# Differential attention in an encoder layer: weights times values as three reduced-precision products on split operands, most of it one unit later

## The chip, the cores and the metric

The kernel runs on one core of a Trainium2 chip. The metric is the device time of one launch in microseconds (us); lower is better. PE is the matmul engine TensorE (PEld its weight loads), ACT is ScalarE, DVE is VectorE, POOL is GpSimd, SP is the queue that issues transfers.

## What is computed

One encoder layer on two sequences of 272 and 1040 tokens (16 meta tokens and 256 or 1024 others). Each layer projects the input, runs a linear recurrence on half of the width and differential attention on the other half, and ends in a projection and a feed-forward part. The change touches only the attention:

```
q, k: 4 heads x 2 components x 64      v: 4 heads x 128
s    = einsum('bqhcd,bkhcd->bhcqk', q, k)
pr   = softmax(s)                      # each component by itself
amap = pr[:, :, 0] - lam * pr[:, :, 1]
o    = einsum('bhqk,bkhe->bqhe', amap, v)
```

## The kernel before

The layer is a row of stages, each a block in which every engine has its own instruction list, written out in program order; engines meet only through semaphores, and a waiting instruction holds up all that stands behind it on its engine. `attention` is one of these stages. It goes through 40 units, each one head and 128 query rows: per head two units of the short sequence (272 keys, "short units") and then eight of the long one (1040 keys, "long units"). Unit k does this:

- **score** (PE, L1949): two components, 64 rows each, into pS0 and pS1, three PSUM banks each; the last 16 keys go to the third bank. It waits until both exponentials of unit k-1 have been read out of pS (`exped`).
- **largest** (DVE, L2039): the negated maximum of each component. **exp** (ACT, L1995): exponential and row sum, from pS to pr.
- **difference** (DVE, L2046, L2047, L2050): two small instructions on the row sums and one over the whole row, pr0 + s * pr1, in place.
- **turn** (PE, L1962): the row is transposed in tiles of 128 keys, in batches: batch 0 is tiles 0 to 3 into pT, batch 2 is tiles 7 and 8 (8 has 16 keys) into pT, batch 1 is tiles 4 to 6 into the free part of pS0's third bank, once exp 0 of the next unit has read it. A short unit has one batch of three tiles.
- **copy** (ACT L1916 for batch 0; DVE L1916 and L1919 for batches 2 and 1): from PSUM to amT.
- **times_v** (PE, L1972): the turned tiles times v, in plain float32, summed in pO. The profile writes such a product as two records. **out_of** (ACT, L2006): pO to o_rows.

POOL works through an independent triangular solve (`substitute`) beside the first three quarters of the stage. Nothing but the two small loads at its start comes by DMA. PE's order is score(k), turn(k-1, 0), times_v(k-1, 0), turn(k-1, 2), turn(k-1, 1), times_v(k-1, 2), times_v(k-1, 1), and then score(k+1). ACT's is the copy of batch 0 of k-1, exp(k, 0), exp(k, 1), out_of(k-1). DVE's is difference(k-1), largest(k, 0), largest(k, 1), the copies of batches 2 and 1 of k-1.

`three_pass` (L220) is a helper that other stages use: both operands are kept as a rounded high part and a rest, both of type float32r, and a product is low*high + high*low + high*high, three matmuls of one record each (L223, L224, L225).

## Time and profile before

| | us |
|---|---|
| median of 3 runs | 2192.63 |
| lowest, highest | 2190.95, 2195.10 |
| the profiled execution, its own time | 2195.91 |
| span of the profile | 2193.9 |

| engine | busy us | share of the span |
|---|---|---|
| PE | 2001.2 | 91% |
| PEld | 1669.4 | 76% |
| DVE | 1411.3 | 64% |
| ACT | 969.2 | 44% |
| POOL | 349.7 | 16% |

The profile shows one execution. Around its span lie 2.0 us that its own time holds as well. Busy time is a sum over stages with different limits, so a share says little on one stage; the rows below are of the attention stage, which lies from about 650 to 926 us, and of a stretch of the projection before it.

### The profile page before, as it was taken

The page shows a single profiled execution, that of the slowest core. Times are in us where ns is not written, and L with a number is a line of the kernel's source. Part 1 is how long each engine was busy: PE and PEld are TensorE (multiplying, and loading weights), DVE is VectorE, ACT ScalarE, POOL GpSimd, SP SyncE. Part 2 cuts the span into 40 slices and gives each one's busy share as a digit, 9 for nine tenths or more (in the row PEclk, how much of TensorE's full clock was granted, in tenths as well). Part 3 has the DMA queues.
Part 4 walks back from the last instruction along what each step waited for, and adds up shares of the span by engine and source line. Part 5 has one row for each costly group of instructions (what it writes and reads, how often), then busy time and mean ns, then how long its engine had stood idle before and what let it go on. Part 6 is the DMA issues. An engine that isn't in the chain of part 4 may idle for free. (4 is left out here: it accounts for less than half of the span.)

```text
span 2193.9 us, 40726 instructions
## 1 busy us (share of the span) xinstructions
PE 2001.2 (91%) x16199; PEld 1669.4 (76%) x16199; DVE 1411.3 (64%) x2299; ACT 969.2 (44%) x1792; POOL 349.7 (16%) x354
## 2 busy tenths in 40 slices
PE   5999999997778888787999698899999999999999
PEld 4666777775555555576887487899999999988887
DVE  5877666673866776655777646756655565557566
ACT  7454467783744444453454322422232232333433
POOL 0000000000019994164554200000000000000000
PEclk8999999998778999958999899899999999999999
DMA  4111155657940001038884534122222222295343
GB/s 179 66 45 54 56 192 203 219 203 245 276 136 1 1 1 58 28 117 170 195 186 115 174 126 142 35 100 93 105 81 87 82 100 81 83 357 168 98 148 109
DMA packets 147287, 269.63 MB, mean 123 GB/s; under 512 B 12992, under 2 KB 85568, under 8 KB 144800
## 3 DMA queue, kind: packets, MB, share of 16 engines
q1 hardware_dynamic: 147104, 267.09, 38.2%
q8 instruction: 127, 2.08, 0.4%
q14 instruction: 56, 0.46, 0.1%
HBM read 172.53 MB, written 91.54 MB: 120 GB/s over the span
## 5 line engine op out<-in xcount | busy, mean ns | idle before, releaser
L2942 DVE TENSOR_TENSOR ff_lefts<-normed_raw,ff_lefts 128x512 fp32r<-128x512 f32 x154 | 105.6, 687 | 97.9 <-ACT ff_lefts L2826 97.7
L225 PE MATMUL ff_acc<-right_t_high,ff_lefts 128*128 128x320 f32 x528 | 163.1, 309 | 0.0
L224 PE MATMUL ff_acc<-right_t_low,ff_lefts 128*128 128x320 f32 x528 | 163.1, 309 | 0.0
L223 PE MATMUL ff_acc<-right_t_high,ff_lefts 128*128 128x320 f32 x528 | 163.1, 309 | 0.0
L223 PE MATMUL ff_acc<-normed_nl 128*128 128x512 f32 x385 | 149.8, 389 | 0.0
L225 PE MATMUL ff_acc<-normed_nl,normed_nh 128*128 128x512 f32 x385 | 149.8, 389 | 0.0
L2826 ACT CAST ff_lefts<-normed_raw 128x512 fp32r<-128x512 f32 x154 | 93.3, 619 | 116.1 <-DMA normed_raw<-in_w_up 56.1
L2852 ACT COPY normed_n<-ff_acc 128x640 f32<-128x640 f32 x66 | 45.9, 695 | 205.6 <-PE ff_acc L225 204.5
L1972 PE MATMUL at_pO<-heads_vt,at_amT 128*128 128x128 f32 (+1 forms) x624 | 104.6, 302 | 35.0 <-ACT at_amT L1916 24.5
L1972 PEld LDWEIGHTS at_pO<-heads_vt,at_amT 128*128 128x128 f32 (+1 forms) x624 | 82.8, 195 | 61.0 <-issue 39.9
L3014 DVE TENSOR_TENSOR normed_nl<-normed_raw,normed_nh 128x640 fp32r<-128x640 f32 x77 | 63.3, 822 | 91.7 <-ACT normed_nh L2875 91.5
L2875 ACT CAST normed_nh<-normed_raw 128x640 fp32r<-128x640 f32 x77 | 56.3, 731 | 144.7 <-PE ff_acc L225 126.2
L223 PE MATMUL ff_acc<-normed_nh,ff_lefts 128*128 128x320 f32 x352 | 109.9, 312 | 7.5 <-DVE ff_lefts L2942 7.5
L223 PE MATMUL pj_acc<-parts_nh,pj_w0rest 128*128 128x512 f32 (+1 forms) x288 | 110.2, 383 | 7.1 <-DVE parts_nl L800 7.1
L2039 DVE TENSOR_REDUCE at_st<-at_pS 128x1 f32<-128x1040 f32 (+1 forms) x80 | 82.7, 1076 | 49.8 <-PE at_pS L1949 49.4
L224 PE MATMUL ff_acc<-normed_nl,ff_lefts 128*128 128x320 f32 x352 | 109.6, 311 | 0.0
L225 PE MATMUL ff_acc<-normed_nh,ff_lefts 128*128 128x320 f32 x352 | 109.6, 311 | 0.0
L223 PE MATMUL pj_acc<-parts_nh,pj_w1rest 128*128 128x512 f32 (+1 forms) x288 | 108.3, 376 | 0.0
L224 PE MATMUL pj_acc<-parts_nl,pj_w0high 128*128 128x512 f32 (+1 forms) x288 | 105.3, 366 | 0.0
L633 ACT COPY pj_raw<-pj_acc 128x512 f32<-128x512 f32 (+1 forms) x72 | 37.4, 523 | 153.4 <-PE pj_acc L225 152.0
L225 PE MATMUL pj_acc<-parts_nh,pj_w0high 128*128 128x512 f32 (+1 forms) x288 | 105.1, 365 | 0.0
L224 PE MATMUL pj_acc<-parts_nl,pj_w1high 128*128 128x512 f32 (+1 forms) x288 | 104.5, 363 | 0.0
(372 smaller groups left out, 5684.5 us busy)
## 6 DMA issues: line engine op xcount, KB each, us to landing
normed_raw<-dram_h SPq DMA_DIRECT2D x77, 320.0 KB, 3.0
ch_ops<-dram_sx SPq DMA_DIRECT2D x88, 256.0 KB, 5.3
dram_sx<-pr_sx SPq DMA_DIRECT2D x16, 1024.0 KB, 4.1
dram_h<-normed_spread_h SPq DMA_DIRECT2D x44, 320.0 KB, 2.3
pj_packed<-in_w_in SPq DMA_DIRECT2D x24, 512.0 KB, 5.0
heads_vt<-dram_sx SPq DMA_DIRECT2D x44, 256.0 KB, 4.9
normed_raw<-in_w_gate SPq DMA_DIRECT2D x22, 512.0 KB, 4.3
normed_raw<-in_w_up SPq DMA_DIRECT2D x22, 512.0 KB
```

The costliest lines, as they stand in the source:

```text
L223: nc.tensor.matmul(out, ll, rh, start=start, stop=False, skip_group_check=onto_kept)
L224: nc.tensor.matmul(out, lh, rl, start=False, stop=False, skip_group_check=onto_kept)
L225: return nc.tensor.matmul(out, lh, rh, start=False, stop=stop, skip_group_check=onto_kept)
L633: nc.scalar.copy(raw[p % 2][:, CUTS[n]:CUTS[n + 1]], acc[bank_of(i)][:, 0:widths[n]]).then_inc(copied, 1)
L1972: last = mm(pO[:, out_cols(k)], amT[k % 2][0:kn, w, :], g.vt[0:kn, h, v0 + w, :], start=(w == 0), stop=(w == tiles_of[k][min(1, batches[k] ...
L2039: nc.vector.reduce_max(st[k % 2][:, x, 0:1], pS[x][:, 0:ln], AX_X, negate=True).then_inc(maxed[x], 1)
L2826: nc.scalar.copy(lefts[:, q % LEFTS, 0, :], raw[:, y, QUARTER[p], :]).then_inc(high, 1)
L2852: nc.scalar.copy(in_two(to), got(y, p)).then_inc(kept, 1)
L2875: nc.scalar.copy(left_high[s], left_raw[s]).then_inc(left_cut, 1)
L2942: tt(lefts[:, q % LEFTS, 1, :], raw[:, y, QUARTER[p], :], lefts[:, q % LEFTS, 0, :].bitcast(F32), ALU.subtract).then_inc(low, 1)
L3014: tt(left_low[s], left_raw[s], left_high[s].bitcast(F32), ALU.subtract).then_inc(left_rest, 1)
```

## The change

- The two amT buffers become am_high and am_low, two of each, in float32r. ACT now takes all batches out of PSUM with a rounding copy into am_high (`high_part`, order 0, 2, 1); DVE then reads the same PSUM tile again and subtracts am_high from it into am_low (`low_part`).
- v is split in the same way, once a head: `cut_v` on ACT, four rounding copies, `rest_v` on DVE, four subtractions.
- `times_v` calls `three_pass`: three matmuls for each tile.
- Batches 2 and 1 of unit k-2 are multiplied behind score(k) and turn(k-1, 0), one unit later than before. Batch 0 of k-1 follows behind them.
- ACT's out_of(k-2) now stands ahead of exp(k, 0). high_part of batches 2 and 1 stands behind exp(k, 1). DVE's low_part(k-1, 0) stands between the two maxima.
- New waits on PE: the last piece of score(k) waits until batch 1 of k-2 is split, turn(k-1, 0) waits until batch 2 of k-2 is split (they share a bank), times_v(k, 0) waits for out_of(k-1) and for v's rest.

```diff
-        amT = [c.sb(f"amT{s}", (P, 9, P)) for s in range(2)]
+        am_high, am_low = ([c.sb(f"{n}{s}", (P, 9, P), F32R) for s in range(2)] for n in ("am_high", "am_low"))
+        v_high, v_low = (c.sb(n, (P, 2, len(VTILES), P), F32R) for n in ("v_high", "v_low"))
...
         def copied(eng, k, b):
-            if b == 0:
-                eng.wait_ge(act_copied, PRIMED + act0[k] + 1)
-            else:
-                eng.wait_ge(tail_copied, PRIMED + dve0[k] + AFTER[b])
+            eng.wait_ge(low_made, PRIMED + bat0[k] + AFTER[b] + 1)
...
                     for lo in range(0, ln, 512):
                         hi = min(lo + 512, ln)
+                        if lo == 1024 and k >= 2 and batches[k - 2] > 1:
+                            copied(pe, k - 2, 1)
...
                     if b == 0:
                         pe.wait_ge(diffed, PRIMED + k + 1)
+                        if k:
+                            copied(pe, k - 1, 2 if batches[k - 1] > 1 else 0)
...
                     if b == 0:
-                        pe.wait_ge(ocopied, PRIMED + k - 1)
+                        pe.wait_ge(ocopied, PRIMED + k)
+                        pe.wait_ge(v_rest, PRIMED + h + 1)
                     copied(pe, k, b)
                     for w in tiles_of[k][b]:
                         kn = min(P, ln - w * P)
-                        last = mm(pO[:, out_cols(k)], amT[k % 2][0:kn, w, :], g.vt[0:kn, h, v0 + w, :],
-                                  start=(w == 0), stop=(w == tiles_of[k][min(1, batches[k] - 1)][-1]))
+                        last = three_pass(nc, pO[:, out_cols(k)], [t[k % 2][0:kn, w, :] for t in (am_high, am_low)],
+                                          [t[0:kn, h % 2, v0 + w, :] for t in (v_high, v_low)],
+                                          w == 0, w == tiles_of[k][min(1, batches[k] - 1)][-1])
...
-                for k in range(1, ALL + 1):
+                for k in range(1, ALL + 2):
                     if k < ALL:
                         score(k)
-                    if k:
+                    if k <= ALL:
                         turn(k - 1, 0)
+                    if k > 1 and batches[k - 2] > 1:
+                        times_v(k - 2, 2)
+                        times_v(k - 2, 1)
+                    if k <= ALL:
                         times_v(k - 1, 0)
                         if batches[k - 1] > 1:
                             turn(k - 1, 2)
                             turn(k - 1, 1)
-                            times_v(k - 1, 2)
-                            times_v(k - 1, 1)
...
+                def high_part(k, b):
+                    act.wait_ge(turned, PRIMED + bat0[k] + AFTER[b] + 1)
                     if b == 0:
                         act.wait_ge(outs, PRIMED + k - 1)
+                    copy_batch(lambda of, got: nc.scalar.copy(of(am_high), got), k, b).then_inc(high_made, 1)
+
+                def cut_v(h):
+                    for of, at in v_runs(h):
+                        last = nc.scalar.copy(v_high[at], g.vt[of])
+                    last.then_inc(v_cut, 1)
...
-                for k in range(ALL + 1):
-                    if k:
-                        turn_copy(k - 1, 0)
+                for k in range(ALL + 2):
+                    if 1 <= k <= ALL:
+                        high_part(k - 1, 0)
+                    if k >= 2:
+                        out_of(k - 2)
                     if k < ALL:
                         exp(k, 0)
                         exp(k, 1)
...
-                    if k:
-                        out_of(k - 1)
+                    if k % NU == 0 and k < ALL:
+                        cut_v(k // NU)
+                    if 1 <= k <= ALL and batches[k - 1] > 1:
+                        high_part(k - 1, 2)
+                        high_part(k - 1, 1)
...
+                def low_part(k, b):
+                    dve.wait_ge(high_made, PRIMED + bat0[k] + AFTER[b] + 1)
+                    copy_batch(lambda of, got: nc.vector.tensor_tensor(of(am_low), got, of(am_high).bitcast(F32), ALU.subtract), k, b
+                               ).then_inc(low_made, 1)
+
+                def rest_v(h):
+                    dve.wait_ge(v_cut, PRIMED + h + 1)
+                    for of, at in v_runs(h):
+                        last = nc.vector.tensor_tensor(v_low[at], g.vt[of], v_high[at].bitcast(F32), ALU.subtract)
+                    last.then_inc(v_rest, 1)
...
                     if k < ALL:
                         largest(k, 0)
+                    if k:
+                        low_part(k - 1, 0)
+                    if k < ALL:
                         largest(k, 1)
...
-                    if k and by_dve[k - 1]:
-                        tail(k - 1)
+                    if k % NU == 0 and k < ALL:
+                        rest_v(k // NU)
+                    if k and batches[k - 1] > 1:
+                        low_part(k - 1, 2)
+                        low_part(k - 1, 1)
```

How this moves PE's instructions, in the inner long units. Digits behind names number the buffers; at_pr10 is the row of the odd units, at_pr00 of the even ones. Before, from turn(k-1, 0) to the first piece of score(k+1):

```order
L1962 MATMUL at_pT<-at_ident,at_pr10 128x128 x4
L1972 MATMUL at_pO<-heads_vt,at_amT1 128x128 x4
L1962 MATMUL at_pT<-at_ident,at_pr10 128x128
L1962 MATMUL at_pT<-at_ident,at_pr10 16x128
L1962 MATMUL at_pS0<-at_ident,at_pr10 128x128 x3
L1972 MATMUL at_pO<-heads_vt,at_amT1 128x128 x5
L1949 MATMUL at_pS0<-heads_kr,heads_qr 128x512
```

Now, from turn(k-1, 2) of an odd unit to the first products behind the next score:

```order
L1968 MATMUL at_pT<-at_ident,at_pr10 128x128
L1968 MATMUL at_pT<-at_ident,at_pr10 16x128
L1968 MATMUL at_pS0<-at_ident,at_pr10 128x128 x3
L1953 MATMUL at_pS0<-heads_kr,heads_qr 128x512
L1953 MATMUL at_pS1<-heads_kr,heads_qr 128x512
L1953 MATMUL at_pS0<-heads_kr,heads_qr 128x512
L1953 MATMUL at_pS1<-heads_kr,heads_qr 128x512
L1953 MATMUL at_pS0<-heads_kr,heads_qr 128x16
L1953 MATMUL at_pS1<-heads_kr,heads_qr 128x16
L1968 MATMUL at_pT<-at_ident,at_pr00 128x128 x4
L223 MATMUL at_pO<-at_v_high,at_am_low1 128x128
L224 MATMUL at_pO<-at_v_low,at_am_high1 128x128
```

The products of a unit's last five tiles (am_low1, am_high1: the odd unit) moved behind the next score and the next unit's first four transposes.

ACT, same place in the program, before (first_y_first is o_rows here, the output of a unit):

```order
L2006 COPY first_y_first<-at_pO 128x128
L1916 COPY at_amT0<-at_pT 128x512
L1995 ACTIVATE at_pr10,first_z0<-at_pS0,at_st1 128x1040
L1995 ACTIVATE at_pr11,at_st1<-at_pS1,at_st1 128x1040
L2006 COPY first_y_first<-at_pO 128x128
```

and now:

```order
L2021 COPY first_y_first<-at_pO 128x128
L2005 ACTIVATE at_pr10,first_z0<-at_pS0,at_st1 128x1040
L2005 ACTIVATE at_pr11,at_st1<-at_pS1,at_st1 128x1040
L2012 CAST at_am_high0<-at_pT 128x128
L2012 CAST at_am_high0<-at_pT 16x128
L2012 CAST at_am_high0<-at_pS0 128x384
L2012 CAST at_am_high1<-at_pT 128x512
L2021 COPY first_y_first<-at_pO 128x128
```

The copy of a unit's output moved from behind the two exponentials to ahead of them, and three more copies stand behind them.

## Rows read from the trace of the kernel before

**Rows 1.** Busy time by stretch: us, engines, PE's granted clock, DMA share, GB/s

```profile
650.00:926.20 276.20, 228.74 (x1352) 154.61 (x1352) 186.88 (x304) 117.47 (x250) 183.20 (x188) 0.93 0.03 13
```

**Rows 2.** PE in time order, one long unit: start, length, instruction, idle before

```profile
686.55 2.12 PE L1949 MATMUL at_pS<-heads_kr,heads_qr 64*128 64x512 f32 x12
688.59 0.66 PE L1962 MATMUL at_pT<-at_ident,at_pr 128*128 128x128 f32 x4
690.02 1.13 PE L1972 MATMUL at_pO<-heads_vt,at_amT 128*128 128x128 f32 x8 [0.77 <-ACT at_amT L1916]
...
691.93 1.77 PE L1972 MATMUL at_pO<-heads_vt,at_amT 128*128 128x128 f32 x10
693.63 2.12 PE L1949 MATMUL at_pS<-heads_kr,heads_qr 64*128 64x512 f32 x12
```

**Rows 3.** ACT in time order, the same unit

```profile
689.29 0.59 ACT L1916 COPY at_amT<-at_pT 128x512 f32<-128x512 f32 x1 [2.37 <-PE at_pT L1962]
689.97 1.13 ACT L1995 ACTIVATE at_pr<-at_pS,at_st 128x1040 f32<-128x1040 f32 x1
691.12 1.13 ACT L1995 ACTIVATE at_pr<-at_pS,at_st 128x1040 f32<-128x1040 f32 x1
692.14 0.19 ACT L1995 ACTIVATION_READ_ACCUMULATOR at_pr<-at_pS,at_st 128x1 f32 x1
693.74 0.27 ACT L2006 COPY first_y_first<-at_pO 128x128 f32<-128x128 f32 x1 [1.40 <-PE at_pO L1972]
```

**Rows 4.** DVE in time order, the same unit

```profile
688.69 2.39 DVE L2039 TENSOR_REDUCE at_st<-at_pS 128x1 f32<-128x1040 f32 x2 [1.34 <-PE at_pS L1949]
691.40 0.29 DVE L1916 COPY at_amT<-at_pT 128x128 f32<-128x128 f32 x1 [0.32 <-PE at_pT L1962]
691.82 0.56 DVE L1916 COPY at_amT<-at_pS 128x384 f32<-128x384 f32 x1
692.44 0.16 DVE L2046 RECIPROCAL at_st<-at_st 128x1 f32<-128x1 f32 x1
692.94 1.41 DVE L2050 SCALAR_TENSOR_TENSOR at_pr<-at_pr,at_st 128x1040 f32<-128x1040 f32 x1
```

**Rows 5.** Weight loads in time order, in the projection stage

```profile
485.00 0.75 PEld L557 LDWEIGHTS pj_pair<-lora_small,pr_q 128*128 128x128 f32 x6
485.67 0.19 PEld L223 LDWEIGHTS pj_acc<-parts_nh,pj_w1rest 128*128 128x128 f32 x1
485.78 0.19 PEld L224 LDWEIGHTS pj_acc<-parts_nl,pj_w1high 128*128 128x128 f32 x1
```

**Rows 6.** PE in time order, three_pass on 288 columns

```profile
486.44 0.30 PE L225 MATMUL pj_acc<-parts_nh,pj_w1high 128*128 128x288 f32 x1
486.58 0.30 PE L223 MATMUL pj_acc<-parts_nh,pj_w1rest 128*128 128x288 f32 x1
```

**Rows 7.** Groups by line and shape: count, busy us, mean ns, idle before

```profile
L2942 DVE TENSOR_TENSOR ff_lefts<-normed_raw,ff_lefts 128x512 fp32r<-128x512 f32 x154 | 105.6, 687 | 97.9 <-ACT ff_lefts L2826 97.7
L2050 DVE SCALAR_TENSOR_TENSOR at_pr<-at_pr,at_st 128x1040 f32<-128x1040 f32 x32 | 49.1, 1533 | 1.1
L804 DVE TENSOR_TENSOR pj_w0rest<-pj_packed,pj_w0high 128x1024 fp32r<-128x1024 f32 x12 | 14.7, 1222 | 11.2 <-ACT pj_w0high L624 11.2
L624 ACT CAST pj_w0high<-pj_packed 128x1024 fp32r<-128x1024 f32 x12 | 12.6, 1046 | 0.0
```

**Rows 8.** Busy time by stretch, columns as in Rows 1: four stretches

```profile
787.59:793.30 5.71, 4.70 (x33) 3.50 (x32) 3.42 (x9) 1.80 (x6) 5.24 (x7) 1.00 0.02 4
793.30:796.23 2.93, 2.23 (x14) 1.37 (x13) 0.92 (x3) 1.72 (x7) 2.69 (x4) 1.00 0.00 0
866.79:877.57 10.78, 10.01 (x40) 6.91 (x40) 6.28 (x11) 2.82 (x6) 0.00 (x0) 0.57 0.01 2
877.57:884.65 7.08, 6.17 (x40) 4.22 (x39) 4.97 (x9) 3.22 (x6) 0.00 (x0) 1.00 0.00 0
```

More of the change, by code:

```diff
@@ L1885, in attention @@
         diffed, outs, ocopied = c.sem("diffed"), c.sem("outs"), c.sem("ocopied")
-        turned, act_copied, tail_copied = c.sem("turned"), c.sem("act_copied"), c.sem("tail_copied")
+        turned, high_made, low_made = c.sem("turned"), c.sem("high_made"), c.sem("low_made")
         tiles_of = [[range(0, 4), range(4, 7), range(7, 9)] if u[3] == LEN_B else [range(0, 3)] for u in units]
         batches = [len(x) for x in tiles_of]
-        by_act = [min(n, 1) for n in batches]
-        by_dve = [n - a for n, a in zip(batches, by_act)]
-        bat0, act0, dve0 = ([sum(x[:k]) for k in range(ALL)] for x in (batches, by_act, by_dve))
+        bat0 = [sum(batches[:k]) for k in range(ALL + 1)]
         row_sum = lambda k, x: st[k % 2][:, 1, 1:2] if x else g.z0[:, units[k][0], k % NU:k % NU + 1]
@@ L1915, in copy_batch, with v_runs @@
             n = full - tiles.start
-            last = copy(amT[k % 2][:, tiles.start:full, :], src[:, 0:n * P].rearrange("p (w t) -> p w t", w=n))
+            at = lambda t, rows, lo, hi: t[k % 2][rows, lo:hi, :]
+            last = copy(lambda t: at(t, slice(0, P), tiles.start, full), src[:, 0:n * P].rearrange("p (w t) -> p w t", w=n))
             if full < tiles.stop:
                 kn = ln - full * P
-                last = copy(amT[k % 2][0:kn, full, :], turned_tile(b, full)[0:kn, :])
+                last = copy(lambda t: at(t, slice(0, kn), full, full + 1), turned_tile(b, full)[0:kn, :].rearrange("p (w t) -> p w t", w=1))
             return last
+        def v_runs(h):
+            return [((slice(0, n), h, slice(w0, w1)), (slice(0, n), h % 2, slice(w0, w1))) for w0, w1, n in VRUNS]
         with nc.Block() as block:
@@ L1996, in exp @@
                                          bias=st[k % 2][:, x, 0:1], accum_out=row_sum(k, x)).then_inc(exped[x], 1)
-                def turn_copy(k, b):
-                    act.wait_ge(turned, PRIMED + bat0[k] + b + 1)
+                def high_part(k, b):
+                    act.wait_ge(turned, PRIMED + bat0[k] + AFTER[b] + 1)
                     if b == 0:
                         act.wait_ge(outs, PRIMED + k - 1)
-                    copy_batch(nc.scalar.copy, k, b).then_inc(act_copied, 1)
+                    copy_batch(lambda of, got: nc.scalar.copy(of(am_high), got), k, b).then_inc(high_made, 1)
[3 more added lines that the diff above has]
+                    last.then_inc(v_cut, 1)
                 def out_of(k):
@@ L2051, in difference @@
                                                    op0=ALU.mult, op1=ALU.add).then_inc(diffed, 1)
-                def tail(k):
-                    for b in (2, 1):
-                        dve.wait_ge(turned, PRIMED + bat0[k] + AFTER[b] + 1)
-                        copy_batch(nc.vector.tensor_copy, k, b).then_inc(tail_copied, 1)
+                def low_part(k, b):
[7 more added lines that the diff above has]
+                    last.then_inc(v_rest, 1)
                 for k in range(ALL + 1):
```

1 line of the change is left out of this document (added).

## Prediction

> **What bounds the stage now.** I read the stretch table first, to see how long the attention stage is and at what clock it runs; then PE, ACT and DVE in time order over one long unit, to see which engine never catches its breath; then, for prices, the groups by line and shape, and the weight loads and narrow matmuls of another stage.
>
> The stage takes some 276 us at a mean clock of 0.93 [rows 1]. In the inner long units it repeats exactly: score starts at 686.55 and again at 693.63, a period of 7.08 us [rows 2]. PE sets it. Its list for one unit is the score (2.04), four transposes, a wait of 0.77 for ACT's copy, eight records of products, five transposes, ten records of products, and the next score starts at once, though both exponentials had been done at 692.33 [rows 2, 3]. ACT waits 2.37 and 1.40 us a unit for PE, DVE 1.34 and 0.32 [rows 3, 4]. So PE's list is the bound, with about 1.4 us of waits and unhidden starts in it, and ACT and DVE have slack. The question is what closes the loop once the products move.
>
> **PE's own work.** A product is now two records, 0.112 us from start to start: eight of them last 1.13 with a tail of 0.16 and an unhidden start [rows 2]. What holds them at 0.112 seems to be the weight load, not the columns: six records of only 2 columns, each with 128 columns of weights, have loads that start (0.75 - 0.19) / 5 = 0.112 apart, and two float32r loads behind one another start at 485.67 and 485.78, also 0.11 apart [rows 5]. At full clock 128 columns stream in 0.053. No float32r matmul in the trace is narrower than 288 columns; those start 0.13 to 0.14 apart, of which 0.12 is their columns [rows 6]. So a three_pass product costs three loads, 0.336, where the plain one costs two, 0.224. Ends: 0.067 a pass (0.053 of columns and the 0.013 that the 288-column pass has over its own), if the load doesn't bind, and 0.14 (the 288-column row). I take 0.112, the row with the same load. PE's work grows by nine tiles x 0.112 = 1.0 us in a long unit, against 1.0 to 1.4 us of waits taken off it. By PE alone the change would be about even.
>
> The Trainium skill (TensorE: Matmul & The Clock Gate, LDWEIGHTS) has the load take the number of weight columns over 1.2 GHz, 107 ns for 128; the 0.112 of the rows agrees, and the rule speaks against the change: three loads for two. The same page (Back-to-back issue gap) gives about 81 ns for each matmul with its load at 128 columns. By that figure, which no row here shows, fifteen passes on the chain below would be 0.47 shorter, the period near 8.3 and the time near 2252.
>
> **The chain that the new order makes.** ACT's out_of(k-2) stands ahead of exp(k, 0) and waits for the end of times_v(k-2, 1), which PE does behind turn(k-1, 0), which waits for difference(k-1), which DVE does behind low_part(k-2, 1), which waits for ACT's high_part(k-2, 1), which stands behind both exponentials of k-1. That is a loop through all three engines, once round per unit:
> - difference: 0.50 from the reciprocal to the long instruction, and that at its mean, 1.53 [rows 4, 7]: 2.03. Its ends are the 1.41 of the row and about 2.2;
> - hand-over 0.05, four transposes 0.50 (0.66 less the tail): 0.55 [rows 2];
> - products of tiles 7, 8 and 4 to 6: 15 x 0.112 = 1.68, a first load that nothing hides and two changes of row count (128, 16, 128), 0.3 together, tail 0.16: 2.14. The 0.3 is my share of the 0.49 that the ten records of before have over 10 x 0.112 + 0.16 [rows 2];
> - out_of: 0.23. Its 0.27 is overlapped at the end [rows 3];
> - two exponentials: 1.15 each from start to start, 2.3 [rows 3];
> - high_part of batches 2 and 1: three short copies, 0.27, about 0.25 and 0.48 by the slope between 0.59 for 512 columns and 0.27 for 128, overlapped, then the hand-over: 0.86 [rows 3]. low_part of batch 2 lies beside the last of them: its two instructions would start the next 0.42 later [rows 4];
> - low_part of batch 1 up to the reciprocal: 0.62, as the copy of 384 columns now [rows 4]. A subtraction of 512 columns takes 0.687, one cycle of DVE a column like the copy [rows 7]; it reads one operand from PSUM and one from SBUF, for which I allow nothing to 0.3.
>
> Sum 8.7 us, against 7.08. The engines' own sums stay under it: PE about 6.7, DVE about 6.1, ACT about 4.8 busy. So the waits that the change takes off PE come back in other places: PE would now idle about 1.3 us ahead of turn(k-1, 0), for DVE. What the added waits hold up: behind PE's wait for difference stand all products, behind ACT's wait for out_of's sum stand both exponentials, behind these the next score. The last piece of score(k) waits for low_part(k-2, 1), but its first four matmuls cover that at 1.7 us. Added writes cost nothing else; no transfer moves.
>
> Six intervals of each of four heads are of this kind: 24 x (8.7 - 7.08) = 39 us.
>
> **Short units and v's split.** From the first short unit's score to the second takes 5.71 now, and to the first long one 2.93 [rows 8]. Behind the first stands now the whole chain up to the products of the last two long units, so it costs nearly a long unit, about 8.3. Into the second goes v's split: ACT's four copies, 1.05 for 1024 columns and about 0.37 and twice 0.25 for the rest, less overlap, 1.65; then DVE's four subtractions, 1.22 and about 0.7 more, 1.9 [rows 7]; then low_part and the short difference behind them: about 8.6. Together 8.3 + 8.6 - 8.64 = +8 a head; ends 4, if half of it hides beside PE's backlog, and 12. The other two intervals keep their time, since what stands in front of them is short. 4 x 8 = 32 us. The last unit's products come one place later and the first head has no long unit in front; I set these against each other.
>
> **Sum**: 39 + 32 = 71. Against the profiled execution's own 2195.9 that is 2267; that execution was 3.3 over the median, so against the median of 2192.6 it is 2264. With every term at its low end (0.067 a pass, DVE undisturbed) the period is 7.8 and the sum 17 + 16 = 33, 2226; at the high end 9.6, 61 + 48 = 109, 2302.
>
> **Rivals.**
> - *The load doesn't bind* (0.067 a pass, the rest as taken): chain 8.05, 23 + 28 = 51, 2244. For it: the 0.112 of float32r loads rests on one pair of rows. Against: six loads with hardly a column beside them at the same 0.112 [rows 5]. Chance 0.10.
> - *The chain doesn't close, and PE's list decides*: should difference(k-1) be ready when score(k) ends, PE would run without waits: 2.05 + 9 x 0.109 + 27 x 0.112 + about 0.6 of starts and row changes = 6.7, 0.4 under now; 28 x 0.4 = 11 less, about 2181, **faster**. It decides at a chain under 6.7; that needs 2 us less on DVE and ACT than their rows give. Chance 0.04, and 0.03 for something between, within 0.2% of now (4.4 us, about what a measurement of this kernel can tell from no change).
> - *A narrow float32r pass is slow*: if a pass under 288 columns needed as long as a whole plain product, 0.223, the chain would have 1.7 more and batch 0's twelve passes, 2.7, would come to stand ahead of the next score: about 11 a unit, +94, and +55 in the short part, some 2340. No row speaks for it but the absence of one narrower than 288. Chance 0.07.
> - *The clock falls*: the same long unit took 10.78 at a granted clock of 0.57 and 7.08 at 1.00 [rows 8]; the low stretch came behind short units, in which PE was less busy. PE will be busy for less of a unit than now. At the lower level of 1.2 GHz PE's list alone is about 13, 4.3 over the chain; a dozen such units add 52 to the forecast, 2316. Chance 0.12.
>
> **How the numbers follow.** The forecast 2264 has 0.64. The range leaves out the slow pass, the faster case and the one within 0.2%, and half of the upper part of the falling clock: 2230 to 2320. Faster 0.04, same 0.03, slower 0.93.
>
> **What would show it.** A period of 8.4 to 9.0 in the inner long units; PE idle ahead of turn on DVE's long instruction; the first exponential waiting for nothing but out_of, and out_of for L225; L223 to L225 on at_pO 0.112 apart; low_part of batch 1 directly ahead of the reciprocal; the two short intervals near 8.5. If out_of finds its products done, the chain is another one. If PE's idle time ahead of turn is small and its records are over 0.15 apart, the narrow pass was the cause.

## The result, and the profile after

| | before | after |
|---|---|---|
| median, us (4 runs each, same chip) | 2193.86 | 2313.81 |
| lowest, highest | 2190.95, 2197.00 | 2301.11, 2322.05 |
| ratio to before, 95% interval | 1 | 1.0533 [1.0500, 1.0566] |
| the profiled execution's own time | 2195.91 | 2301.11 |
| its span | 2193.9 | 2299.3 |

The changed kernel is slower by 120 us, 5.3%. The forecast was 2264, the range 2230 to 2320. A second measurement of the same changed kernel (below) gave 2316.4. The profiled execution is the shortest of its four, 12.7 under the median.

First the stretch that answers to [rows 1]: the attention stage of after, from the first score to the first instruction of the next stage. The columns are us, busy time and instructions of PE, PEld, DVE, ACT and POOL, PE's granted clock, DMA share, GB/s.

```profile
648.46:1028.40 379.94, 310.71 (x1664) 234.26 (x1664) 215.80 (x369) 144.61 (x363) 180.19 (x189) 0.74 0.02 10
```

The stage took 379.9 us where it took 275.7 before (first score at 650.71, next stage at 926.4): +104.2, and the two spans differ by 105.4. So the loss is all here. Its mean clock fell from 0.93 to 0.74.

PE in time order over one long unit at full clock, to hold against [rows 2] (two stretches; "..." leaves out products):

```profile
690.73 2.12 PE L1953 MATMUL at_pS<-heads_kr,heads_qr 64*128 64x512 f32 x12 [0.20 <-ACT at_pr L2005]
693.61 0.66 PE L1968 MATMUL at_pT<-at_ident,at_pr 128*128 128x128 f32 x4 [0.76 <-DVE at_pr L2070]
694.02 0.31 PE L223 MATMUL at_pO<-at_v_high,at_am_low 128*128 128x128 f32 x1
...
695.12 0.27 PE L224 MATMUL at_pO<-at_v_low,at_am_high 128*128 128x128 f32 x1
695.23 0.27 PE L225 MATMUL at_pO<-at_v_high,at_am_high 128*128 128x128 f32 x1
695.34 0.28 PE L223 MATMUL at_pO<-at_v_high,at_am_low 128*128 128x128 f32 x1
...
696.53 0.33 PE L223 MATMUL at_pO<-at_v_high,at_am_low 128*128 128x128 f32 x1 [0.35 <-ACT first_y_first L2021]
...
698.85 2.11 PE L1953 MATMUL at_pS<-heads_kr,heads_qr 64*128 64x512 f32 x12 [0.20 <-ACT at_pr L2005]
```

ACT in the same unit, and the start of the next round on DVE (to hold against [rows 3, 4]):

```profile
696.21 0.27 ACT L2021 COPY first_y_first<-at_pO 128x128 f32<-128x128 f32 x1 [1.32 <-PE at_pO L225]
696.38 1.14 ACT L2005 ACTIVATE at_pr<-at_pS,at_st 128x1040 f32<-128x1040 f32 x1
...
697.49 1.13 ACT L2005 ACTIVATE at_pr<-at_pS,at_st 128x1040 f32<-128x1040 f32 x1
...
698.59 0.40 ACT L2012 CAST at_am_high<-at_pT 128x128 fp32r<-128x128 f32 x2
```

```profile
691.77 0.14 DVE L2066 RECIPROCAL at_st<-at_st 128x1 f32<-128x1 f32 x1
...
692.25 1.30 DVE L2070 SCALAR_TENSOR_TENSOR at_pr<-at_pr,at_st 128x1040 f32<-128x1040 f32 x1
...
699.02 0.48 DVE L2075 TENSOR_TENSOR at_am_low<-at_pT,at_am_high 128x128 fp32r<-128x128 f32 x2 [2.26 <-ACT at_am_high L2012]
699.43 0.54 DVE L2075 TENSOR_TENSOR at_am_low<-at_pS,at_am_high 128x384 fp32r<-128x384 f32 x1
699.89 0.14 DVE L2066 RECIPROCAL at_st<-at_st 128x1 f32<-128x1 f32 x1
```

This is the chain of the prediction, link by link: reciprocal 691.77, turn 693.61, first product 694.02, out_of 696.21, first exponential 696.38, high part 698.59, low part of batch 1 699.43, reciprocal again 699.89. The links are 1.84, 0.41, 2.19, 0.17, 2.21, 0.84 and 0.46, in sum 8.12, and the score-to-score interval is 8.12 too. ACT goes from out_of straight into both exponentials, and out_of waits for L225. Every engine on this chain has idle time, and none of them sets the pace alone (POOL is busy for 7.65 of the 8.12, but nothing here waits for its results).

The next unit shows the rest. Here the stretches are the unit above, the whole next one, and its part before and behind 705.00:

```profile
690.73:698.85 8.12, 6.81 (x48) 5.38 (x49) 5.57 (x9) 3.73 (x11) 7.65 (x7) 1.00 0.01 2
698.85:709.21 10.36, 8.52 (x48) 6.91 (x48) 6.38 (x10) 4.00 (x11) 9.58 (x11) 0.80 0.00 1
701.34:705.00 3.66, 2.55 (x19) 2.29 (x19) 3.44 (x4) 0.59 (x1) 3.47 (x3) 1.00 0.00 0
705.00:709.21 4.21, 3.85 (x18) 3.43 (x17) 0.68 (x2) 2.91 (x7) 3.82 (x6) 0.50 0.00 0
```

```profile
702.45 0.66 PE L1968 MATMUL at_pT<-at_ident,at_pr 128*128 128x128 f32 x4 [1.48 <-DVE at_pr L2070]
...
705.86 0.41 PE L225 MATMUL at_pO<-at_v_high,at_am_high 128*128 128x128 f32 x1
706.08 0.41 PE L223 MATMUL at_pO<-at_v_high,at_am_low 128*128 128x128 f32 x1
706.29 0.41 PE L224 MATMUL at_pO<-at_v_low,at_am_high 128*128 128x128 f32 x1
```

PE had idled 1.48 us for DVE, whose long instruction took 2.02 instead of 1.30 (last section). From 705 on the granted clock was 0.50, and a pass needed 0.21 from start to start instead of 0.11. The unit took 10.36.

Worked out from the starts of the scores, the two stages compare like this (us, rounded from the starts; head 0 has no long unit ahead of it and is kept apart):

| intervals | before | after | difference | forecast |
|---|---|---|---|---|
| the 23 from inner long units | 162.8 | 201.2 | +38.3 | +37 |
| the two short ones, heads 1 to 3 | 25.9 | 68.2 | +42.3 | +24 |
| the two behind them, heads 1 to 3 | 44.7 | 52.3 | +7.5 | 0 |
| the first four of head 0 | 28.8 | 34.0 | +5.2 | +8 |
| last score to the next stage | 13.4 | 24.4 | +10.9 | +2 |
| stage | 275.7 | 379.9 | +104.2 | +71 |

In this execution six of the 23 inner intervals are at full clock throughout, with a mean of 8.17; the other 17, partly at the lower level, have 8.95.

### The profile page after: what moved, and what is told of

The parts are those of the page before. It is cut to its first block and busy times, and to the rows that moved or that the text cites. A ratio compares the mean times of both kernels' runs of the same rounds, so it can differ in the third digit from the quotient of the medians.

```text
span 2299.3 us, 41568 instructions
## 1 busy us (share of the span) xinstructions
PE 2078.8 (90%) x16511; PEld 1745.3 (76%) x16511; DVE 1441.1 (63%) x2363; ACT 997.5 (43%) x1904; POOL 347.5 (15%) x354
## 5 line engine op out<-in xcount | busy, mean ns | idle before, releaser
L225 PE MATMUL ff_acc<-right_t_high,ff_lefts 128*128 128x320 f32 x528 | 163.1, 309 | 0.0
L225 PE MATMUL ff_acc<-normed_nl,normed_nh 128*128 128x512 f32 x385 | 149.8, 389 | 0.0
L223 PE MATMUL at_pO<-at_v_high,at_am_low 128*128 128x128 f32 (+1 forms) x312 | 105.7, 339 | 24.5 <-DVE at_am_low L2075 13.5
L1953 PE MATMUL at_pS<-heads_kr,heads_qr 64*128 64x512 f32 (+2 forms) x416 | 103.7, 636 | 12.8 <-ACT at_pr L2005 8.6
L225 PE MATMUL ff_acc<-normed_nh,ff_lefts 128*128 128x320 f32 x352 | 109.6, 311 | 0.0
L2012 ACT CAST at_am_high<-at_pT 128x512 fp32r<-128x512 f32 (+3 forms) x112 | 35.8, 360 | 166.7 <-PE at_pT L1968 166.7
L225 PE MATMUL pj_acc<-parts_nh,pj_w0high 128*128 128x512 f32 (+1 forms) x288 | 105.1, 365 | 0.0
```

The source lines that it names most:

```text
L223: nc.tensor.matmul(out, ll, rh, start=start, stop=False, skip_group_check=onto_kept)
L225: return nc.tensor.matmul(out, lh, rh, start=False, stop=stop, skip_group_check=onto_kept)
L1953: last = mm(pS[x][:, lo:hi], g.qr[rows, h, q0:q0 + P], g.kr[rows, h, a + lo:a + hi], start=True, stop=True)
L2012: copy_batch(lambda of, got: nc.scalar.copy(of(am_high), got), k, b).then_inc(high_made, 1)
```

## Experiments

Each ratio is to the kernel before in runs on the same chip; the medians are from several chips, so compare by the ratios. delay_only and turn2_first are changes to the kernel before, the others to the kernel after. Interval and clock figures are of the profiled execution of each kernel; intervals run from score to score.

| kernel | median | ratio, 95% interval | stage, us | clock in it | long unit at full clock |
|---|---|---|---|---|---|
| before | 2193.86 | | 275.7 | 0.93 | 7.08 |
| after | 2313.81 | 1.0533 [1.0500, 1.0566] | 379.9 | 0.74 | 8.12 |
| after_again | 2316.40 | 1.0533 [1.0503, 1.0563] | 394.2 | 0.69 | 8.13 |
| delay_only | 2211.15 | 1.0062 [1.0043, 1.0081] | 284.7 | 0.90 | 6.88 |
| plain_products | 2271.43 | 1.0341 [1.0312, 1.0370] | 350.8 | 0.82 | 7.71 |
| three_in_place | 2425.02 | 1.1043 [1.1007, 1.1079] | 493.6 | 0.59 | none |
| no_read | 2289.88 | 1.0425 [1.0390, 1.0459] | 364.0 | 0.73 | 7.44 |
| v_once | 2303.01 | 1.0496 [1.0459, 1.0533] | 378.7 | 0.73 | 8.13 |
| filler | 2301.04 | 1.0488 [1.0458, 1.0518] | 381.2 | 0.87 | 8.23 |
| filler_long | 2308.15 | 1.0494 [1.0450, 1.0538] | 383.5 | 0.79 | 8.23 |
| turn2_first | 2185.52 | 0.9958 [0.9942, 0.9973] | 261.6 | 0.94 | 6.75 |

### after_again: the same kernel once more

> The changed kernel itself once more, as the measure for the runs beside it. It took 2301 to 2322 us. Its long units take 8.12 us where the granted clock is 1.00 and POOL is idle, 8.5 to 8.9 beside POOL, and 10.3 where the clock is low; the mean clock of the attention stage was 0.74 against 0.93 before. Theory A (the chain through three engines gives about +71 us, the clock the rest): the runs differ with the mean clock, the low-clock runs being the long ones.

No edit. The stretch of the stage, and of one of its long units:

```profile
653.42:1047.60 394.18, 330.86 (x1664) 247.34 (x1664) 217.19 (x368) 145.46 (x362) 178.94 (x188) 0.69 0.02 9
818.97:829.34 10.37, 10.02 (x50) 7.24 (x49) 5.73 (x10) 3.98 (x9) 9.74 (x9) 0.66 0.00 0
```

The same instructions took 394.2 us against 379.9, with the clock at 0.69 against 0.74. Where the clock stays full a unit takes the same, 8.13, and six of the 23 inner intervals are of that kind again. Nine of the 23 inner intervals are over 10.3, at mean clocks of 0.66 to 0.80, where the first profile had two. PE's clock is what differs: DVE's busy time grew by 1.4 us, PE's by 20. So nearly all of the 14.3 us is the clock, between two executions of one program. The long unit at a mean clock of 0.66 has both levels in it, and PE was busy for 10.02 of its 10.37: there PE's list sets the pace, no longer the chain.

### delay_only: the later place of the products alone

```diff
...
-                for k in range(1, ALL + 1):
+                for k in range(1, ALL + 2):
                     if k < ALL:
                         score(k)
-                    if k:
+                    if k <= ALL:
                         turn(k - 1, 0)
+                    if k > 1 and batches[k - 2] > 1:
+                        times_v(k - 2, 2)
+                        times_v(k - 2, 1)
...
+                    if k >= 2:
+                        out_of(k - 2)
                     if k < ALL:
                         exp(k, 0)
                         exp(k, 1)
...
-                    if k:
-                        out_of(k - 1)
```

> The kernel before with the delay alone: batches 2 and 1 are multiplied one unit later, out_of(k-2) stands ahead of the exponentials, with the waits that need it; products stay plain float32 and the copies stay as they were (ACT batch 0, DVE the others). Theory A (the splits behind both exponentials and the third load make the chain long, the delay as such costs nothing): long units of 6.7 to 7.1 us, clock 0.9 or more, time 2185 to 2200 us. Rival D (the delay itself, with out_of ahead of the exponentials, is what costs): over 7.5 us a long unit and over 2210 us.

Plain products and the copies of the kernel before, in the order of the kernel after, with its waits. The long unit got shorter, 6.88 for 7.08; but the two short intervals of heads 1 to 3 took 38.8 us where they took 25.9.

```profile
725.30:734.30 9.00, 7.47 (x31) 6.06 (x32) 2.83 (x8) 1.80 (x6) 8.03 (x13) 0.62 0.00 0
734.30:739.40 5.10, 3.84 (x25) 2.72 (x24) 2.27 (x8) 1.73 (x7) 4.71 (x6) 1.00 0.00 0
830.97:837.85 6.88, 5.91 (x40) 4.38 (x40) 5.15 (x10) 3.08 (x6) 6.49 (x6) 1.00 0.00 0
```

The interval of the second row was 2.93 before [rows 8], at full clock too: the short units now have the products of the last two long ones to wait for. The end takes 18.3 for 13.4, since the last products come one place later. So the delay by itself gives 0.2 us in a long unit and takes back more at the changes of head and at the end. The sum is a small loss, 0.6%, of the 5.3%. It fits neither side of the expectation: the unit is the one of theory A, the time, 2211, the one of rival D.

### plain_products: the split without the third pass

```diff
-                        last = three_pass(nc, pO[:, out_cols(k)], [t[k % 2][0:kn, w, :] for t in (am_high, am_low)],
-                                          [t[0:kn, h % 2, v0 + w, :] for t in (v_high, v_low)],
-                                          w == 0, w == tiles_of[k][min(1, batches[k] - 1)][-1])
+                        last = mm(pO[:, out_cols(k)], am_high[k % 2][0:kn, w, :].bitcast(F32), g.vt[0:kn, h, v0 + w, :],
+                                  start=(w == 0), stop=(w == tiles_of[k][min(1, batches[k] - 1)][-1]))
```

> The changed kernel, with its splits, waits and order, but each product is one plain float32 matmul of the high part and the unsplit values; what is left out is the low part's product. 18 loads a long unit for 27. Theory A: the chain is shorter by 5 x 0.112 = 0.56 us, so long units take 7.6 to 8.3 us at full clock; PE waits more, so the clock of the stage stays low, 0.7 to 0.85; time 2240 to 2285 us. Rival B (the float32r passes lower the clock): the clock is 0.9 or more and the time near 2225 us.

All copies and subtractions stay; the product is the plain one of two records, and the low part's product is left out.

```profile
871.20:878.91 7.71, 5.97 (x39) 4.37 (x40) 5.58 (x9) 3.72 (x11) 0.00 (x0) 1.00 0.00 0
```

With delay_only and after on its two sides this splits the long unit: 7.08, less 0.20 for the delay, plus 0.83 for high and low parts in place of copies, plus 0.41 for the third pass. The medians go 2196, 2211, 2271, 2316 (before, delay_only, plain_products, after_again, one chip): +15, +60, +45. So half of the loss comes with the high and low parts (v's among them) on ACT and DVE, which both hand each batch on within the loop. Of the 66 us that they add to the stage of delay_only, 21 lie in the 23 inner intervals and 36 in the four intervals at each change of head.

The third pass costs more than its place in the chain. From plain_products to after_again the inner intervals grew from 182.2 to 214.1 us, by 31.8; 23 x 0.41 is 9.4 of that. The rest goes with the clock. With plain products 21 of the 23 inner intervals ran at full clock, with three passes six:

```profile
855.69:902.07 46.38, 35.88 (x236) 26.18 (x235) 33.52 (x54) 22.37 (x54) 0.00 (x0) 1.00 0.00 1
```

These are the six inner intervals of head 2, with PE busy for 77% of them. The same six of after_again have the clock at 0.77 and PE busy for 93%, in part because its work is longer at the lower level:

```profile
878.67:935.55 56.88, 52.83 (x289) 39.50 (x288) 34.12 (x55) 23.36 (x54) 0.00 (x0) 0.77 0.00 1
```

So in the inner units it isn't PE's idle time alone that brings the lower level. The rival of the expectation, that the float32r passes themselves bring it, fits these units; it asked for 0.9 and 2225 over the whole stage, and at the changes of head the clock fell with plain products too (0.72 and 0.64 in the two short intervals of head 1).

### three_in_place: three passes without the delay

```diff
...
-                        turn(k - 1, 0)
-                    if k > 1 and batches[k - 2] > 1:
-                        times_v(k - 2, 2)
-                        times_v(k - 2, 1)
...
+                    turn(k - 1, 0)
+                    times_v(k - 1, 0)
+                    if batches[k - 1] > 1:
+                        turn(k - 1, 2)
+                        turn(k - 1, 1)
+                        times_v(k - 1, 2)
+                        times_v(k - 1, 1)
...
                         high_part(k - 1, 2)
                         high_part(k - 1, 1)
+                    if k:
+                        out_of(k - 1)
```

> The split and the three products as in the changed kernel, but in the order of the kernel before: all products of unit k-1 behind its transposes, out_of at the end of ACT's list, no unit later. Theory: the three products lie behind high and low part of batch 1, and these behind the second exponential, so PE waits longer still: a warm long unit of about 9.2 to 9.7 and 2335 to 2380 with the clock. Rival (the later place of the products is what costs, through the wait for out_of): a warm long unit under 8.1 and a time under 2300.

```profile
943.62 4.03 PE L1951 MATMUL at_pS<-heads_kr,heads_qr 64*128 64x512 f32 x12
947.58 1.12 PE L1964 MATMUL at_pT<-at_ident,at_pr 128*128 128x128 f32 x4
950.18 0.30 PE L223 MATMUL at_pO<-at_v_high,at_am_low 128*128 128x128 f32 x1 [1.49 <-DVE at_am_low L2068]
...
953.29 0.47 PE L223 MATMUL at_pO<-at_v_high,at_am_low 128*128 128x128 f32 x1 [1.01 <-DVE at_am_low L2068]
```

```profile
847.73:862.32 14.59, 12.73 (x50) 9.44 (x49) 5.76 (x9) 4.08 (x9) 0.00 (x0) 0.50 0.00 0
```

The unit took 13.45 at a mean clock of 0.63, and no inner unit ran at full clock. The direction was as expected, the size was above it (2335 to 2380): the score took 4.03 instead of 2.12, PE had two waits of 1.49 and 1.01 for low parts in each unit, and it had the lower level for part of every inner unit. A few, as the one of the last row, had it throughout: there PE's list is 12.73 and the unit 14.59. For three passes the later place is therefore right: it is worth about 110 us (ratios of 1.1043 and 1.0533), with what the clock adds. It doesn't make good what the split costs.

### no_read: out_of waits for nothing

```diff
                 def out_of(k):
-                    act.wait_ge(outs, PRIMED + k + 1)
-                    nc.scalar.copy(g.o_rows[:, units[k][0], k % NU, :], pO[:, out_cols(k)]).then_inc(ocopied, 1)
+                    nc.scalar.copy(g.o_rows[:, units[k][0], k % NU, :], ident[:, :]).then_inc(ocopied, 1)
```

> The changed kernel, but out_of copies a tile that is in SBUF (the identity) and waits for nothing, so o_rows does not get the product. Work on every engine stays the same. Theory (the loop closes through ACT's wait for the last product of unit k-2 ahead of the exponentials): the warm long unit falls from 8.12 to about 7.4 where POOL is idle, PE's wait for DVE's long instruction ahead of the turn shrinks from about 0.8 to 0.1-0.4 us, the stage gets 20 to 50 us shorter (the clock follows), 2265 to 2295. Rival (the waits are set by ACT's and DVE's own amount of work, the place of out_of does not matter): the warm long unit stays within 0.15 of 8.12 and the time within 8 us of 2314.

```profile
882.96 2.12 PE L1953 MATMUL at_pS<-heads_kr,heads_qr 64*128 64x512 f32 x12
885.86 0.66 PE L1968 MATMUL at_pT<-at_ident,at_pr 128*128 128x128 f32 x4 [0.78 <-DVE at_pr L2069]
```

```profile
887.24 1.13 ACT L2005 ACTIVATE at_pr<-at_pS,at_st 128x1040 f32<-128x1040 f32 x1
...
889.04 1.13 ACT L2005 ACTIVATE at_pr<-at_pS,at_st 128x1040 f32<-128x1040 f32 x1 [0.59 <-DVE at_st L2058]
```

This kernel leaves out reading the product: o_rows gets the identity. The unit fell to 7.44 and the time to 2289.9, both as the theory said: the wait for the last product ahead of the exponentials does close the loop, and is worth 0.68 us a unit. (The edit also frees PE's own wait for out_of, 0.35 in after; but behind that PE still waited 0.20 for the exponentials there, so it wasn't on the chain.) One part of the expectation failed. PE's wait ahead of the turn stayed at 0.78; what gave way was a wait of 0.59 on ACT that came up between the two exponentials, for DVE's second maximum. So behind this loop stands another one, over DVE's list of maxima, low part and difference, only 0.7 shorter. Moving out_of behind the exponentials in earnest wasn't tried: PE would then write the bank of pO while ACT reads it, which the kernel's waits avoid, and its PSUM tiles fill all eight banks.

### v_once: v split for the first head only

```diff
...
-                    if k % NU == 0 and k < ALL:
+                    if k == 0:
                         cut_v(k // NU)
...
-                    if k % NU == 0 and k < ALL:
+                    if k == 0:
                         rest_v(k // NU)
```

> The changed kernel with v split for head 0 only; the other heads use head 0's split v, so their output is another. It takes ACT's four copies and DVE's four subtractions out of three heads. Theory (v's split lies on the path, between the two short units): the interval from the second short unit's score to the next shrinks by about 2 us at full clock, 2 to 4 at the lower level; 8 to 12 us in all, 2302 to 2306. Rival (it hides beside PE's backlog of products): under 3 us, 2311 to 2314.

Heads 1 to 3 use head 0's split v here and do without their own. The ratio is 1.0496 against 1.0533, about 8 us less, but the intervals overlap, so the gain is not shown. By place the theory is mostly wrong. The interval that holds the split fell by 2.8 us in head 1 (12.79 to 10.00, both at a clock of 0.50), but by only 0.35 in heads 2 and 3 (9.53 to 9.18, against after_again). There PE, at the lower level, came late with its transposes anyhow, and the split lay beside that; DVE waited for high parts instead. What head 1 has more is POOL at work (last section). What else differs is not on the split's interval, and I can't tell it from a difference of the clock.

### filler and filler_long: keeping PE busy

```diff
                     if b == 0:
-                        pe.wait_ge(diffed, PRIMED + k + 1)
                         if k:
                             copied(pe, k - 1, 2 if batches[k - 1] > 1 else 0)
+                        for i in range(4 if ln == LEN_B else 12):
+                            mm(pT[:, 0:P], g.vt[:, 0, 3, :], g.vt[:, 0, 4, :], start=True, stop=True)
+                        pe.wait_ge(diffed, PRIMED + k + 1)
```

> The changed kernel with extra matmuls on PE ahead of turn(k-1, 0), where PE waits for DVE: 4 plain ones for a long unit, 12 for a short one, whose results nothing reads. Theory A (PE's waits lower the granted clock, and that is what the forecast missed): the clock of the stage goes back to 0.9 or more, the long units stay at 8.2 to 8.9, the stage gets shorter although work was added, and the whole takes 2255 to 2280 us. Rival B (the float32r passes, which stream 128 columns in half the time of a weight load, lower the clock, whatever PE does while it waits): the clock stays near 0.75 and the time is that of the changed kernel or 10 to 20 us more. Rival C (the clock costs little, the chain is simply longer than forecast): the clock goes up and the time stays within 10 us of the changed kernel.

```profile
876.36:884.58 8.22, 7.68 (x56) 6.31 (x57) 5.57 (x9) 3.72 (x11) 0.00 (x0) 1.00 0.01 2
830.38:838.25 7.87, 6.49 (x49) 5.43 (x49) 3.97 (x9) 3.47 (x12) 7.25 (x9) 1.00 0.01 2
838.25:850.15 11.90, 8.68 (x56) 7.81 (x55) 5.92 (x16) 2.87 (x12) 3.79 (x7) 0.86 0.62 264
```

```profile
841.84 4.43 PE L1964 MATMUL at_pT<-heads_vt 128*128 128x128 f32 x24 [2.86 <-DVE at_am_low L2077]
```

filler_long has 0 in place of 12.

> The changed kernel with four plain matmuls of 128 columns, whose results nobody reads, on PE ahead of the wait for the difference in long units only; they lie in PE's idle time of 1.3 us. The first filler run also had twelve in each short unit, where they cost time of their own. Theory (part of the loss is the clock, which falls where PE idles): granted clock in the stage 0.80 to 0.88 against 0.69-0.74, the stage 8 to 20 us shorter, 2292 to 2306, with the warm long unit at 8.1 to 8.3. Rival (the clock falls behind the short units whatever the long ones do, or the fillers lie on the path): clock under 0.77 or the time within 5 us of 2314 or above.

In filler the mean clock of the stage rose from 0.69 and 0.74 to 0.87, and eleven of the 23 inner intervals ran at full clock instead of six. The stage took 381.2, near the 379.9 of the first profile of after and 13 below the 394.2 of the second. The medians on one chip say the same: 2301.0 against 2316.4 for after_again, 15 us less (four runs of 2299 to 2309 against four of 2309 to 2320; the intervals of the two ratios overlap a little). That is far from the 2255 to 2280 of theory A and just outside the 10 us of rival C. Rival B, by which the clock stays near 0.75 whatever PE does while it waits, is out in that form: with the same passes the fillers raised the clock. The fillers take 0.9 us of PE in a long unit and fit into the idle time there only at full clock (8.23 for 8.12); at the lower level they lie on PE's list. The twelve of a short unit lie on the path: in the last row they, 24 records, take 4.43 us ahead of a short unit's transposes, and that interval (the third row above) has 11.90 at 0.86, where after had 9.95 at 0.50. The second row is the first short interval of head 2 at full clock: 7.87, where after had 12.26 at 0.50.

filler_long brought the clock to 0.79, just short of what the theory asked, and its median, 2308, lies between the two theories; its runs spread from 2297 to 2314. So a higher mean clock that is bought with work on the same engine gave back about 15 of the 120 us at best, and neither run gives a price of the clock by itself.

Here is how the kernels stand in the inner units (PE's busy time in a long unit at full clock; three_in_place has none, so its unit at 0.63 is given):

| kernel | products | PE busy in the unit, us | inner intervals of 23 at full clock |
|---|---|---|---|
| before | plain | 6.17 of 7.08 | 23 |
| turn2_first | plain | 6.06 of 6.75 | 23 |
| delay_only | plain | 5.91 of 6.88 | 22 |
| plain_products | plain | 5.97 of 7.71 | 21 |
| after, after_again | three passes | 6.81 of 8.12 | 6, 6 |
| no_read | three passes | 6.59 of 7.45 | 7 |
| v_once | three passes | as after | 4 |
| filler | three passes and plain fillers | 7.68 of 8.22 | 11 |
| filler_long | three passes and plain fillers | as filler | 7 |
| three_in_place | three passes | 10.95 of 13.45 | 0 |

PE has most idle time at full clock in plain_products, which kept that clock, and less in after and no_read, which did not. So idle time alone doesn't set the clock, and, by filler, the passes alone don't either; but the widest gap in these runs lies between the kinds of product. plain_products and after differ in the product alone, but with it the length of a unit and the places of PE's waits change too, and no run separates these from the passes themselves.

### turn2_first: from the kernel before, the other way

```diff
                     if k:
                         turn(k - 1, 0)
-                        times_v(k - 1, 0)
                         if batches[k - 1] > 1:
                             turn(k - 1, 2)
+                        times_v(k - 1, 0)
+                        if batches[k - 1] > 1:
                             turn(k - 1, 1)
```

turn(k, 2) also waits until ACT has copied batch 0.

> The kernel before with one thing moved: on PE, turn(k-1, 2) stands ahead of times_v(k-1, 0) instead of behind it, with a wait for ACT's copy of batch 0, which lies in the same columns of pT. DVE can then take its copy of batch 2 about 0.9 us sooner. Theory (PE's list is the bound in the kernel before, and the last wait in it is for DVE's copies ahead of the last ten records): the long unit falls from 7.08 by 0.05 to 0.2, 2 to 5 us in all, 2190 to 2194 beside a before of about 2195. Rival (PE only swaps one list for another and the copies were in time): the unit stays at 7.08 and the ratio within 0.1% of 1.

```profile
758.99:765.74 6.75, 6.06 (x40) 4.23 (x39) 5.32 (x9) 3.22 (x6) 6.36 (x6) 1.00 0.01 2
```

```profile
762.36 0.44 PE L1964 MATMUL at_pT<-at_ident,at_pr 128*128 128x128 f32 x2 [0.68 <-ACT at_amT L1916]
762.64 1.06 PE L1974 MATMUL at_pO<-heads_vt,at_amT 128*128 128x128 f32 x8
...
764.06 1.75 PE L1974 MATMUL at_pO<-heads_vt,at_amT 128*128 128x128 f32 x10
```

This one beats both kernels: 0.9958 [0.9942, 0.9973], 11 us under before on the same chip, a small gain but clear of the noise. The long unit is 6.75 for 7.08, more than the 0.05 to 0.2 expected. The wait for ACT (0.68 now, 0.77 in [rows 2]) stands ahead of two transposes instead of ahead of the products. Batch 2 is turned when DVE comes out of its maxima, and DVE's copy of it follows them without the 0.32 of idle time that [rows 4] have there, so that the last ten records can start sooner:

```profile
761.13 2.39 DVE L2042 TENSOR_REDUCE at_st<-at_pS 128x1 f32<-128x1040 f32 x2 [0.95 <-PE at_pS L1949]
763.44 0.28 DVE L1916 COPY at_amT<-at_pT 128x128 f32<-128x128 f32 x1
```

The bound of the kernel before was PE's list with its waits, as the prediction read it, and the gain lay in one of these waits.

## Why the prediction was right in part

- **The chain was right.** It closes where the prediction said, through the links it named. Its sum was 8.7, measured 8.12 with POOL idle or little in its way and 8.4 beside it; so the 8.4 to 9.0 named as the sign was not met at full clock. The terms that were too long, forecast for measured: the difference (2.03 for 1.84, hand-over included; I took the mean of the long instruction, 1.53, and it took 1.30 in this unit), the transposes (0.55, there with the hand-over, for 0.41), low_part of batch 1 (0.62 for 0.46). The products were 2.14 for 2.19, out_of 0.23 for 0.17, the exponentials 2.3 for 2.21, the high parts 0.86 for 0.84. no_read shows that the loop is this one. Of the engines' own sums PE's was 6.81 for 6.7, DVE's 5.57 for 6.1, ACT's 3.73 for 4.8.
- **A pass at 0.112 was right** at full clock. The rivals with the unbound load and with the slow narrow pass are out.
- **PE's wait ahead of the turn** was said to be 1.3 and was 0.76 and 1.48 in the two units shown.
- **The step that failed is the clock.** The sum priced every unit at full clock, and put the case of a falling clock at 0.12. It came in every profile of this kernel: 0.74 and 0.69 for the stage. The price given there, 2316, is what was measured (2313.8 and 2316.4), but by luck. The upper end of the sum's own terms was 2302, under both; the range held them because half of this case was left in it. The prediction had a dozen long units wholly at the lower level, 4.3 each, 52 in all, on top of its forecast. Its 13 for PE's list at that level was right: three_in_place has 12.73 in a unit at 0.50 throughout. But no inner unit of after had the lower level throughout: those over 10.3 had mean clocks of 0.66 to 0.80 and cost 2.24 (10.37 for 8.13), and over all inner units it came to 13 us in one execution and 26 in the other. A good part of the loss is at the change of head instead: in heads 1 to 3 both short intervals ran at 0.50 throughout and took 11.7 to 12.3 and 9.5 to 12.8 us, where 8.3 and 8.6 were forecast for full clock.
- **The reason given for a falling clock is not enough.** It was that PE would be busy for less of a unit. PE is busy for 84% of a long unit of after and 87% of one before, which fits; but plain_products has 77% and kept full clock in 21 of 23 inner intervals, and no_read has 88% and kept it in seven. What the runs show beside the fall is three passes in place of plain products, and fillers, which leave PE less idle time, took back a part of it. The prediction priced a slower narrow pass, which there isn't; it did not ask what the passes do to the clock.
- **The +38.3 of the inner units agree with the forecast by accident.** At full clock throughout they would be 23 x (8.17 - 7.08) = 25; the clock added 13, and as much again in the second execution. What the clock took in all can't be read directly. An estimate for the first execution, without the first head and the end, is 13 for these and, by filler's 7.87 at full clock against after's 11.7 to 12.3, about 4 for each of three first short intervals: about 25 of the 104.
- **The first head and the end don't cancel.** They were set against each other. The head's first four intervals gave +5.2 instead of +8, the end +10.9 instead of +2: behind the last score the chain has to be gone through twice, the second time for products that were delayed.
- **v's split was placed right and mostly mis-priced**: of the 3.5 taken for it, 2.8 in head 1 and near 0.35 in heads 2 and 3.

What stays open is why three passes come with a lower granted clock than plain products do, why the clock at the same place in the same program differs from execution to execution, and so how much of a run's time is due to it.

## What to carry to other kernels

A product in more passes has to pay for the splitting of its operands. Whether it pays where one split serves many products, no run here shows. Here each row of weights is used once, so each split is one more trip through ACT and DVE for each product, and these trips come to lie in the loop. Before putting work "one unit later", follow the loop once round through all engines, at the change of problem size as well, and look for an in-order engine that waits for the late result ahead of what the next unit needs. And price the lower clock as part of the sum, not as a side case, where a change alters PE's idle time or the kind of its products.

## What the runs showed of the hardware

- **DVE and POOL slow each other down.** v's low part reads two operands from SBUF on DVE. The four subtractions of one head took 4.43 us in head 1 and 1.95 in head 3. Here they are, in head 1 with POOL at work and in head 3 with POOL done:

```profile
745.95 4.43 DVE L2081 TENSOR_TENSOR at_v_low<-heads_vt,at_v_high 128x256 fp32r<-128x256 f32 x4 [4.68 <-ACT at_v_high L2016]
...
933.42 1.95 DVE L2081 TENSOR_TENSOR at_v_low<-heads_vt,at_v_high 128x256 fp32r<-128x256 f32 x4 [4.68 <-ACT at_v_high L2016]
```

```profile
747.91 2.33 POOL L1036 TENSOR_TENSOR at_inverses<-at_inverses,at_solve_tmp 128x512 f32<-128x512 f32 x1
...
751.48 1.17 POOL L1036 TENSOR_TENSOR at_inverses<-at_inverses,at_solve_tmp 128x510 f32<-128x510 f32 x1
```

Beside the first, a POOL instruction took 2.33 where its neighbour of nearly the same size took 1.17. The long instruction of difference, with two SBUF operands as well, took 2.02 beside POOL at 700.38; the 1.30 of 692.25, beside POOL too, is what it never exceeds once POOL is done, so not every one is caught.

```profile
700.38 2.02 DVE L2070 SCALAR_TENSOR_TENSOR at_pr<-at_pr,at_st 128x1040 f32<-128x1040 f32 x1
```

The low parts, which read one operand from PSUM, have 0.69 for 512 columns in both units (at 694.92 and 703.76). The Trainium skill (SBUF — State Buffer, SBUF: two separate sides) has the two engines take turns at one pair of ports for whole instructions, when DVE has two operands in SBUF and POOL reads SBUF; these rows agree, and the rows of low_part are what it would leave undisturbed.
- **A pass doubles at the lower level.** Its starts are 0.112 apart at full clock and 0.213 at 0.50, so what holds it at 0.112 is no time that stays when the clock falls. The prediction took the weight load for it; the rows don't settle how load and columns share the 0.112.
- **One program, one place, two clocks.** after and after_again run the same instructions; the four intervals from the scores of units 16 to 19 took 8.12, 9.83, 8.86 and 8.66 us in one, and 8.13, 11.48, 10.37 and 10.37 in the other.
